# Dealing the rows of the expert weights to the partitions in blocks of neighbours

## The reference, cut to what matters

```python
def moe_swiglu(h, w_router, w_g, w_u, w_d):
    t = h.reshape(-1, D_MODEL)                      # 256 tokens in two calls of 128
    logits = (t @ w_router).astype(jnp.float32)
    top_v, top_i = lax.top_k(logits, TOP_K)         # 2 of 8
    top_w = jax.nn.softmax(top_v, axis=-1)
    gate = jnp.sum(jax.nn.one_hot(top_i, N_EXPERTS) * top_w[..., None], axis=1)
    out = jnp.zeros_like(t)
    for e in range(N_EXPERTS):
        out = out + gate[:, e:e + 1] * swiglu(t, w_g[e], w_u[e], w_d[e])
    return out.reshape(shp)
# swiglu(h, w_g, w_u, w_d) = (silu(h @ w_g) * (h @ w_u)) @ w_d
# w_g, w_u: 1024 x 3584 for each expert; w_d: 3584 x 1024
```

## Time and profile before

| | us |
|---|---|
| median of 3 runs | 1837.43 |
| lowest, highest | 1836.29, 1838.24 |
| the profiled execution | 1836.77 |
| its span | 1834.9 |
| TensorE (PE) busy | 1718.0 (94%) |
| VectorE (DVE) busy | 610.7 (33%) |
| ScalarE (ACT) busy | 516.7 (28%) |
| GpSimd (POOL) busy | 93.3 (5%) |
| granted TensorE clock, mean | 0.971 |

### The profile page before, as it was taken

One profiled execution on the slowest core, in us unless ns is written; L12 is line 12 of the kernel. 1 busy time (PEld: TensorE's weight loads), 2 busy tenths in 40 slices (PEclk: granted clock), 3 DMA queues, 4 the chain that ended last, 5 costly groups with the idle time before them and its releaser, 6 DMA issues.

```text
span 1834.9 us, 31874 instructions
## 1 busy us (share of the span) xinstructions
PE 1718.0 (94%) x14271; PEld 1063.7 (58%) x14271; DVE 610.7 (33%) x1021; ACT 516.7 (28%) x823; POOL 93.3 (5%) x106
## 2 busy tenths in 40 slices
PE   4999998999998999987999988999999799988997
PEld 2899986999998799987333423333333233323333
DVE  2387675544445478685200000101111010100101
ACT  2445543433343445532100111112121111111111
POOL 3020041000000010040000000000000000000000
PEclk8999998999999999997999999999999999998998
DMA  9364586677764454337587899999999999999990
GB/s 347 119 236 144 207 299 214 226 275 275 265 241 151 164 184 149 139 138 280 189 302 290 323 394 394 394 394 392 391 389 392 394 394 395 393 394 394 393 377 31
DMA packets 229844, 525.68 MB, mean 286 GB/s; under 512 B 5172, under 2 KB 11522, under 8 KB 229712
## 3 DMA queue, kind: packets, MB, share of 16 engines
q1 hardware_dynamic: 227456, 519.68, 76.7%
q0 software_dynamic: 2256, 4.01, 0.9%
HBM read 521.93 MB, written 1.74 MB: 285 GB/s over the span
## 4 chain that ended last, share of the span: by engine, by line
PE 76%; DMA 6%; SPq 6%; DVE 6%; issue 2%; ACT 2%; POOL 1%; POOLq 0%; DVEq 0%; ACTq 0%
PE ps L1955 12%; PE ps L2001 10%; PE ps L1533 10%; PE ps L1535 9%; PE ps L1534 9%; SPq L501 6%; PE ps L1942 5%; DMA raw<-in_w_e_gate_dram 4%; PE ps L1961 4%; PE ps L1949 4%; PE ps L1539 3%; PE ps L2017 2%; PE ps L1597 2%; DVE wlo L945 2%; PE ps L1914 1%
## 5 line engine op out<-in xcount | busy, mean ns | idle before, releaser
L1533 PE MATMUL ps<-acts_hi,whi 128*128 128x256 f32 x1600 | 462.7, 289 | 18.5 <-DVE wlo L945 5.6
L1535 PE MATMUL ps<-acts_hi,wlo 128*128 128x256 f32 x1600 | 454.1, 284 | 0.0
L1534 PE MATMUL ps<-acts_lo,whi 128*128 128x256 f32 x1600 | 454.0, 284 | 0.0
L1533 PEld LDWEIGHTS ps<-acts_hi,whi 128*128 128x128 f32 x1600 | 308.2, 193 | 38.2 <-issue 25.0
L945 DVE TENSOR_TENSOR wlo<-raw,whi 128x1024 fp32r<-128x1024 f32 (+1 forms) x220 | 264.7, 1244 | 191.9 <-ACT whi L623 191.7
L1534 PEld LDWEIGHTS ps<-acts_lo,whi 128*128 128x128 f32 x1600 | 308.3, 193 | 0.8 <-issue 0.7
L1535 PEld LDWEIGHTS ps<-acts_hi,wlo 128*128 128x128 f32 x1600 | 308.2, 193 | 0.0
L623 ACT ACTIVATE whi<-raw 128x1024 fp32r<-128x1024 f32 (+1 forms) x220 | 219.6, 1049 | 81.3 <-DMA raw<-in_w_ff_gate_dram 33.7
L1949 PE MATMUL ps<-raw,KTt 128*32 128x512 f32 x384 | 169.2, 597 | 5.5 <-DMA raw<-in_w_e_gate_dram 5.5
L1494 DVE TENSOR_TENSOR big<-ps,big 96x512 f32<-96x512 f32 x28 | 19.2, 687 | 408.5 <-ACT big L870 408.5
L1955 PE MATMUL ps<-e_raw,KTt 128*32 128x512 f32 x1056 | 154.0, 592 | 0.0
(11 more groups left out here) (307 smaller groups left out, 2030.6 us busy)
## 6 DMA issues: line engine op xcount, KB each, us to landing
e_raw<-in_w_e_down_dram SPq DMA_DIRECT2D x40, 2048.0 KB, 19.2
raw<-in_w_e_up_dram SPq DMA_DIRECT2D x32, 2048.0 KB, 19.4
e_raw<-in_w_e_gate_dram SPq DMA_DIRECT2D x32, 2048.0 KB, 18.0
raw<-in_w_ada_dram SPq DMA_DIRECT2D x24, 2048.0 KB, 8.2
raw<-in_w_e_gate_dram SPq DMA_DIRECT2D x24, 2048.0 KB, 17.1
e_raw<-in_w_e_up_dram SPq DMA_DIRECT2D x24, 2048.0 KB, 19.2
raw<-in_w_in_dram SPq DMA_DIRECT2D x22, 2048.0 KB, 8.9
raw<-in_w_e_down_dram SPq DMA_DIRECT2D x16, 2048.0 KB, 19.2
```

What stands on the lines that cost most here:

```text
L1533: mm(out, a_hi, b_hi, start=start, stop=False, skip_group_check=shared)
L1534: mm(out, a_hi, b_lo, start=False, stop=False, skip_group_check=shared)
L1535: return mm(out, a_lo, b_hi, start=False, stop=stop, skip_group_check=shared)
```

## The change

The place of a weight row changes from k x 128 + p to p x 8 + k for `up` and `gate` and to p x 4 + k for `down`: a partition gets neighbouring rows. So that the products stay the same, the token channels are written to `h2tok` in the matching order (L855: the write steps by 128 elements from one element to the next, in runs of 8), and the hidden product to `e_hidden` likewise (L1497: steps of 128 elements, runs of 4). With three strips the sum of L1494 goes to `up_part` in place of `e_hidden`, so that L1497 doesn't read what it writes. Counts of instructions, buffers, waits and the order of all programs stay.

```diff
-                    sp.dma_start(e_load(kind, ch)[1], src.rearrange("a (k p) n -> p (a k) n", p=P))\
+                    sp.dma_start(e_load(kind, ch)[1], src.rearrange("a (p k) n -> p (a k) n", p=P))\
                         .then_inc(e_landed[j % E_SLOTS], 16)
...
-                act.activation(h2tok[:, b // 2, 512 * (b % 2):512 * (b % 2) + 512], ps[:, 4 + b, :], ACT.Copy)\
+                half = slice(64 * (b % 2), 64 * (b % 2) + 64)
+                act.activation(h2tok[:, b // 2, :].rearrange("t (k q) -> t q k", k=KT)[:, half, :],
+                               ps[:, 4 + b, :].rearrange("t (q k) -> t q k", k=KT), ACT.Copy)\
                     .then_inc(h2_kept, 1)
...
+            def four(a):
+                return a.rearrange("r (q k) -> r q k", k=4)
+
...
                     if S == 3:
-                        tt(e_hidden[0:rows, :], up, up_part[0:rows, :], ALU.add).then_inc(up_sum, 1)
+                        tt(up_part[0:rows, :], up, up_part[0:rows, :], ALU.add).then_inc(up_sum, 1)
                         dve.wait_ge(up_sum, u * CHUNKS + (ch + 1))
-                        up = e_hidden[0:rows, :]
-                    tt(e_hidden[0:rows, :], up, e_gate[0:rows, :], ALU.mult).then_inc(e_hid, 1)
+                        up = up_part[0:rows, :]
+                    tt(e_hidden[0:rows, :].rearrange("r (k q) -> r q k", k=4), four(up), four(e_gate[0:rows, :]),
+                       ALU.mult).then_inc(e_hid, 1)
```

## The result

| us | before | after |
|---|---|---|
| median | 1837.85 | 1831.83 |
| lowest, highest | 1836.08, 1840.10 | 1828.29, 1836.29 |
| the profiled execution | 1836.77 | 1832.15 |
| its span | 1834.9 | 1830.3 |

The ratio of after to before, measured side by side, is 0.9969 with an interval of 0.9963 to 0.9976, 5.7 us less. The forecast was 1830.4.

The account below looks back on a forecast made before the run. The prediction took the DMA transfer rate to bound the kernel from about 1045 to 1690 us. Its terms, 8.1 - 0.6 - 0.35 = 7.1 us saved, gave 1830.4 us, with a range of 1822 to 1842.

Parts of the forecast that it names:

- Part 3: Buffers where two 3-strip items follow one another: late load issues leave a gap, losing 0.6 us, bounds 0 and 1.5.
- Part 1: Loads of `down` in the gapless stretch: 16 KB packets, 4.93 us a load instead of 5.13, 8.1 us saved over 40.
- Rival A: Loads of `down`: the queue still cuts at each row, so pieces aren't joined; 1837.4 to 1838 us, chance 0.20.
- Rival B: Loads of `down`: a packet costs less, part of the difference being address order; if half, 1833.8 us, chance 0.07.
- Part 2: Loads of `up` and `gate`: same packets, only address order changes; 0, bounded by 0.1 us a load, 8 us either way.
- Rivals C and D: `up` and `gate` loads 0.1 us faster each, 1822.5, chance 0.09 (C); 5% slower, 1852, or half, 1841, chance 0.12 (D).
- Part 4: Strided product (L1497): 0.35 us longer, hidden under 1.36 us of cover except at the first item's first chunk, losing 0.35.
- Rival E: Strided product (L1497) outlasts its cover from 2.05 us on and holds up PE; at 2.75 us, 1835, chance 0.04.
- Part 5: Four copies to `h2tok` (L855): the last two, doubled, add 1.08 us ahead of Exp; nothing lost, at most 0.1.
- The tail: From the eighth item's first gate landing to the end: still 144.4 us of PE, ACT and DVE work, loads no longer deciding.
- The sum: Whole kernel: 8.1 - 0.6 - 0.35 = 7.1 us off the profiled execution's 1836.77, giving 1829.7, or 1830.4 as median.

Follow-up runs that it names:

- down alone: Kernel before with only the loads of `down` in the new row order, with its strided product; `up`, `gate`, `h2tok` unchanged: 1833.68 against 1837.16 us, ratio 0.998.

## Why the prediction was right, step by step

The forecast lies 1.4 us under the median, and the mechanism is the one forecast. Two sizes were off, and a part outside the change took some. By the interval of the ratio the gain is 4.4 to 6.8 us where 7.1 were forecast: a little too large, on the side of the two terms that cost more than thought (Part 3) or weren't thought of (the clock's drop at 822 us). That the profiled executions show 4.6 us and the medians 6.0 is the luck of which executions were profiled.

**Part 1, the downs: right.** 4.93 us forecast, 4.93 measured (4.91 at the trace's own resolution); 205,952 packets forecast and read. Rival A (pieces not joined) falls with the packets. Rival B (half of it the order of addresses) falls with the cut to 4 KB, which brings back 5.14 us with the new addresses. The rule of the Trainium skill (DMA: Bandwidth & Descriptors, Why small descriptors are slow), by which a packet costs about 3 cycles, would have made it 0.09 us a down, an estimate; no run here agrees: it was 0.20, and 8 KB pieces lie on the same line.

**Part 2, up and gate: right.** 0 forecast; 5.41 us after and 1.0004 for that half alone. Rivals C and D fall, within far less than the 0.1 us a load by which I had bounded them. That half was 0.21 of the chances and was the widest part of the range. Loads of the same piece size from other spacings told as much beforehand, and could have been trusted more.

**Part 3, the buffers: the term that was mis-sized.** The place and the kind were right (a gap where two items of 3 strips follow one another), the size was not: 0.6 us forecast, 2.2 measured in the trace of the change (559.72 us for the five items where 5 x 111.5 = 557.5 was due), beyond its bound of 1.5. The repeat of the same kernel has 558.9, so 1.4, within the bound; in both it is more than twice the forecast. The step that failed is "it must be issued 2.4 us ahead to leave no gap". That took 7.8 us, the landing of a load on an idle queue, less 5.40. In this place it lands 9.3 us after its issue, and with a lead of 2.87 there is a hole of 1.0; the subtraction gives 3.9 as the lead it needs. The up issued at 1336.60, 2.9 us ahead, brings another hole of 1.1 in the load behind it, while three gates between them, issued 3.5 to 4.0 us ahead, land 5.40 behind their ups. So 2.9 was too little, and 3.5 looks enough.

The other half of the error is that I looked for one tightest place in the trace of before. There were more, which came in turn as the stream moved ahead (1268 to 1276, 1336 to 1340): once TensorE's pace bounds a pair of items, every further tenth is lost there. A bound by pace was missing. TensorE's own time from the third item's first turn (1141.02) to the fourth's (1261.14) is 120.1 us, with gather and scatter, where the faster loads of an item take 111.5. It has no wait from its start on the third item to the fifth item's fifth gate:

```profile
1126.93 0.59 PE L1955 MATMUL ps<-raw,KTt 128*32 128x512 f32 x1 [0.78 <-DMA raw<-in_w_e_gate_dram]
...
1411.42 0.62 PE L1967 MATMUL ps<-e_raw,KTt 128*32 128x512 f32 x2 [0.50 <-DMA e_raw<-in_w_e_gate_dram]
```

In the kernel before the second of these starts at 1411.47: at the end of this run of TensorE's own work nothing of the gain is left, and what the kernel keeps comes from the loads behind it. The drop of the clock at 822 us has a part in that: TensorE starts on the third item 0.9 us later than before (1126.01).

**Part 4, the strided product: right.** It lasts 1.09 us instead of 0.69. In the timeline of VectorE, after:

```profile
1216.94 0.69 DVE L1499 TENSOR_TENSOR big<-ps,big 96x512 f32<-96x512 f32 x1 [14.24 <-ACT big L872]
1217.66 1.10 DVE L1502 TENSOR_TENSOR big<-big 96x512 f32<-96x512 f32 x1
```

and two turns in the chain:

```profile
1203.64 0.48 PE ps L1545 x4
...
1219.71 0.48 PE ps L1545 x4
```

It ends at 1218.76 and the turn starts at 1219.71, so of 1.36 us of cover 0.95 are left, and the cadence is 16.07 us as before. I took 0.35 us; it was 0.40, just over half of the doubling that bounded it. Rival E, from 2.05 us on, falls. The waits of PE between 868 and 1700 us show the one place with no cover, 1.3 us where the earlier trace rows have 0.9, and the loads of gate still waited for:

```profile
PE ps L1967 <- DMA e_raw<-in_w_e_gate_dram: 16.5, 5, 5.8
PE ps L1967 <- DMA raw<-in_w_e_gate_dram: 12.9, 4, 4.7
...
PE ps L1545 <- DVE big L1502: 1.3, 1, 1.3
```

The Trainium skill (Vector Engine (DVE) Microarchitecture Reference, Measured stream behaviour on trn2) gave an estimate of 0.33 us for this; the trace has 0.40.

**Part 5, the copies to `h2tok`: right, with little to spare.** The last two, on ScalarE, and the copy on VectorE behind them:

```profile
863.46 1.90 ACT L856 ACTIVATE big<-ps 128x512 f32<-128x512 f32 x2 [2.93 <-PE ps L1545]
...
868.26 0.17 DVE L1402 COPY qk<-ps 128x16 f32<-128x16 f32 x1 [0.28 <-PE ps L1910]
```

The two take 1.90 us instead of 1.08. VectorE's idle time for PE shortly after, the cover, has shrunk from 1.05 to 0.28. Nothing was lost, but at twice that addition something would have been.

**The tail.** Forecast 144.4 us from the eighth item's first gate to the end. PE starts on it at 1686.45 after, which leaves 143.9, and at 1690.67 before, 144.2.

**The sum.** The spans differ by 4.6 us where 7.1 were forecast. 1.6 us more went into the pair, 1.5 into the load issued later ahead of the experts, where the granted clock was 0.57 in place of 1.00 and which was in no part of the forecast, and 0.6 came back elsewhere, 0.4 of it from the eighth item's first up on. The medians differ by 6.0, since the profiled execution of before lies 1.1 us under its median and that of after 0.3 over.

## What to carry to other kernels

When a stream of equal loads bounds a kernel, read its landings by the size of piece; if two sizes are there, the cost of a packet can be read, and here the gain of joining rows was forecast within 0.02 us a load. Then ask which stretch another engine paces at nearly the stream's rate, since there the gain stops: compare that engine's own time over the whole stretch with the new time of its loads, not the lead at one place. Leave the permutation to an engine with cover (an element-wise write that gets 60% longer behind 1.36 us of slack is free), and not to the weight reads of the one that carries the chain.

## What was not expected of the hardware

- Reading float32 weights with a step of 4 elements makes a weight load of 128 columns 1.5 times as long (141 to 214 ns); with a step of 8 an item's gather takes 7.89 us instead of 3.74, and with it the granted clock was 0.91 in one stretch and 0.96 in another, where it is 1.00 without.
- A strided write costs ScalarE more than VectorE: a copy of 512 elements goes from 0.59 to 1.05 us, a product of 512 from 0.69 to 1.09.
- A load of 2 MB, issued 2.9 us before the last one ahead of it landed, lands 8.9 (down alone) to 9.3 us after its issue, where one alone took 7.8.
- A load of 156 KB on POOL's queue beside the stream takes 6.1 to 7.0 us or 9.0, by the order and the pieces of the big loads.
- A drop of the granted clock to its lower level for 3.4 us, in nine of thirteen traces around 822 us and in four not, delays all loads of the experts behind the second by 1.5 us. It comes with either order of the rows, and before any `down` is issued.
